# Forgetting attention with two value products a head, and denominators from probabilities summed on VectorE

## What is computed

```python
def fox_prompt(q, k, v, logf):
    c = jnp.cumsum(logf, axis=1)
    ...
        s = jnp.einsum('bqhd,bkhd->bhqk', qi, k).astype(jnp.float32) * ATTN_SCALE
        s = s + (ci[..., None] - cT[:, :, None, :])
        s = jnp.where((kpos[None, :] <= qpos[:, None])[None, None], s, NEG_INF)
        p = jax.nn.softmax(s, axis=-1)
        return jnp.einsum('bhqk,bkhd->bqhd', p.astype(v.dtype), v)
```

## Time and profile before

| what | value |
|---|---|
| median of 3 runs | 1436.95 us (1433.86 to 1438.11) |
| the profiled execution | 1437.47 us, of it span 1435.5 us |
| mean granted TensorE clock | 0.993 of full |
| PE busy | 1390.7 us, 97% |
| DVE busy | 577.2 us, 40% |
| ACT busy | 480.7 us, 33% |
| POOL busy | 213.2 us, 15% |

### The profile page before, as it was taken

How to read it: one execution, slowest core, us unless ns; L and a number is a source line. 1 busy time by engine, 2 the same in 40 slices (tenths; PEclk the granted TensorE clock), 3 DMA queues, 4 the chain that set the end, 5 groups by cost and what they waited for, 6 DMA issues and landing times.

```text
span 1435.5 us, 22601 instructions
## 1 busy us (share of the span) xinstructions
PE 1390.7 (97%) x9041; PEld 1289.6 (90%) x9041; DVE 577.2 (40%) x1378; ACT 480.7 (33%) x1049; POOL 213.2 (15%) x317
## 2 busy tenths in 40 slices
PE   6999999999999799999999999999999999999997
PEld 5989898778888677889999999999999999999997
DVE  6345634232323433563333333343424252525156
ACT  6356655655554552553212121212121212111103
POOL 3145541634343230000000000000000000000000
PEclk9999999999999899999999999999999999999999
DMA  7621125212030443314211120202020202020003
GB/s 197 116 67 38 32 85 160 68 42 79 31 101 8 153 163 132 109 49 118 59 45 48 41 62 28 74 16 74 16 74 16 74 16 74 17 76 20 22 1 121
DMA packets 110255, 97.64 MB, mean 68 GB/s; under 512 B 15936, under 2 KB 96928, under 8 KB 109640
## 3 DMA queue, kind: packets, MB, share of 16 engines
q1 hardware_dynamic: 110152, 96.20, 22.9%
HBM read 77.07 MB, written 19.21 MB: 67 GB/s over the span
## 4 chain that ended last, share of the span: by engine, by line
PE 90%; DVE 3%; DMA 3%; ACT 2%; issue 2%; POOL 1%; SPq 0%; DVEq 0%; ACTq 0%
PE ps L594 27%; PE ps L595 26%; PE ps L596 26%; PE ps L798 2%; PE ps L728 1%; PE ps L945 1%; DMA cb<-c_scratch 1%; PE ps L766 1%; PE ps L810 1%; PE ps L675 1%; DMA ob<-o_scratch 1%; DVE ps L1629 1%; PE ps L889 1%; ACT sp_x L1263 0%; PE ps L608 0%
## 5 line engine op out<-in xcount | busy, mean ns | idle before, releaser
L1876 DVE TENSOR_TENSOR outs<-outs,ps 128x384 f32<-128x384 f32 (+1 forms) x264 | 134.6, 510 | 107.9 <-PE ps L596 107.6
L1862 DVE TENSOR_TENSOR gu<-ps,sg 128x384 f32<-128x384 f32 (+1 forms) x66 | 34.6, 525 | 237.2 <-PE ps L596 237.2
L2046 POOL TENSOR_TENSOR pl_x<-sp_x,ph_x 128x512 fp32r<-128x512 f32 (+5 forms) x120 | 102.0, 863 | 174.4 <-ACT sp_x L1263 172.7
L1443 ACT ACTIVATE h_hi<-gu 128x384 fp32r<-128x384 f32 (+1 forms) x66 | 32.9, 498 | 221.8 <-DVE gu L1862 221.8
L1262 ACT ACTIVATE ph_x<-ps,negc 128x512 fp32r<-128x512 f32 (+5 forms) x120 | 63.0, 525 | 84.3 <-PE ps L810 84.3
L1437 ACT ACTIVATE sg<-ps 128x384 f32<-128x384 f32 (+1 forms) x66 | 30.5, 465 | 171.7 <-PE ps L596 171.7
L594 PE MATMUL ps<-f_hi,ff0hi 128*128 128x384 f32 (+1 forms) x264 | 85.7, 325 | 0.0
L594 PE MATMUL ps<-f_hi,ff1hi 128*128 128x384 f32 (+1 forms) x264 | 85.6, 324 | 0.0
L594 PE MATMUL ps<-f_hi,ff3hi 128*128 128x384 f32 (+1 forms) x264 | 85.6, 324 | 0.0
L594 PE MATMUL ps<-f_hi,ff2hi 128*128 128x384 f32 (+1 forms) x264 | 85.6, 324 | 0.0
L595 PE MATMUL ps<-f_lo,ff0hi 128*128 128x384 f32 (+1 forms) x264 | 85.2, 323 | 0.0
(11 more groups left out here) (311 smaller groups left out, 3775.1 us busy)
## 6 DMA issues: line engine op xcount, KB each, us to landing
raw<-in_w_gate SPq DMA_DIRECT2D x22, 512.0 KB, 4.9
raw<-in_w_up SPq DMA_DIRECT2D x22, 512.0 KB, 4.8
raw<-in_w_down SPq DMA_DIRECT2D x22, 512.0 KB, 4.2
raw<-in_w_in SPq DMA_DIRECT2D x14, 512.0 KB, 4.1
cb<-c_scratch SPq DMA_DIRECT2D x4, 1312.0 KB, 7.4
xt<-in_x_prompt SPq DMA_DIRECT2D x8, 512.0 KB, 4.3
out<-outb SPq DMA_DIRECT2D x16, 256.0 KB, 3.2
ob<-o_scratch SPq DMA_DIRECT2D x16, 256.0 KB, 3.0
```

The lines of the kernel that those rows point to most:

```text
L1443: act.activation(h_hi[par][:, f, c0:c0 + n], gu[(f + c) % 2][:, 0:n], ACT.Copy).then_inc(S["g_hi"], 1)
L1862: dve.tensor_tensor(gu[(f + c) % 2][:, 0:n], bank(3 + c, n), sg[c][:, 0:n], ALU.mult)\
L1876: add = dve.tensor_tensor(y, y, bank(b, whole * P).rearrange("p (t m) -> p t m", t=whole), ALU.add)
L2046: pool.tensor_tensor(pl_x[at][0:rows, 0:n], sp_x[at][0:rows, 0:n], ph_x[at][0:rows, 0:n].bitcast(F32), ALU.subtract).then_inc(S["x_pl"], 1)
```

## The change

The value tile `vw` now has five slots of 64 columns per block: lo values of head 0, hi of head 0, zeros, hi of head 1, lo of head 1. A head's product is two matmuls: its hi and lo slots side by side with `ph_x`, and its hi slot beside the zeros with `pl_x`. Each half of the output rows then holds a part of the same sum, and the two halves are added after the turn, by a reduction on VectorE in place of L1607 and L1611.

The denominators come another way. VectorE adds the full probabilities of all blocks of a chunk in `sum_x` (`fox_sum`, one instruction a head and unit). At a chunk's end ScalarE rounds the sums (`sum_hi`), VectorE forms their remainder (`sum_lo`), and in step j = 4, 12 or 0, part 3, TensorE multiplies both with a 128x128 tile of ones into banks 4 and 5 (`fox_denominators`, four products a chunk; the item "dn"). VectorE takes the reciprocal of the whole banks (`fox_inverses`, 128 by 512 for a head in chunks 0 and 1), and multiplies banks 6 and 7 by it into `ot_x` (`fox_out`, now on VectorE). GpSimd now waits for `fox_sum` instead of the exponential.

```diff
+        if v >= 1 and v <= NX and j in (0, 4, 12):
+            minima(("x", v, 3), "dn", (v - 1) // NFU, {4: 0, 12: 1, 0: 2}[j])
...
+        elif p[0] == "dn":
+            waits.append(("x_rd", 2 * (3 * p[1] + p[2] + 1)))
...
-        (vw_hi, vw_lo), end = lay(outs_at + 4 * D, ("vw_hi", [P, 11, 3, HD], F32R), ("vw_lo", [P, 11, 3, HD], F32R))
+        (vw,), end = lay(outs_at + 4 * D, ("vw", [P, 11, 5, HD], F32R))
+        vw_hi, vw_lo = vw[:, :, 1:4:2, :], vw[:, :, 0:5:4, :]
...
-                    vh, vl = (x[0:rows, vb, h:h + 2, :].rearrange("p s d -> p (s d)") for x in (vw_hi, vw_lo))
+                    both, one = (vw[0:rows, vb, s:s + 2, :].rearrange("p s d -> p (s d)") for s in (3 * h, 1 + h))
                     xh, xl = (x[2 * (v % 2) + h][0:rows, 0:n] for x in (ph_x, pl_x))
-                    product(ps[:, 6 + h, at:at + n], vh, vl, xh, xl, first, last).then_inc(S["x_pv"], 1)
+                    out = ps[:, 6 + h, at:at + n]
+                    pe.matmul(out, both, xh, start=first, stop=False)
+                    pe.matmul(out, one, xl, start=False, stop=last).then_inc(S["x_pv"], 1)
+
+            def fox_denominators(i, c):
+                n, at = FCH[c][1], fox_chunk(i, c)
+                for name, value in bank_free(("dn", i, c)):
+                    pe.wait_ge(S[name], value)
+                pe.wait_ge(S["x_sl"], at + 1)
+                for h in range(2):
+                    pe.matmul(ps[:, 4 + h, 0:n], ones_x[:], sum_hi[:, h, 0:n], start=True, stop=False)
+                    pe.matmul(ps[:, 4 + h, 0:n], ones_x[:], sum_lo[:, h, 0:n], start=False, stop=True)\
+                      .then_inc(S["x_dn"], 1)
...
-            def fox_out(v):
+            def fox_sums_hi(v):
...
+                act.wait_ge(S["x_sum"], 2 * (v + 1))
+                if at >= 1:
+                    act.wait_ge(S["x_dn"], 2 * at)
+                act.activation(sum_hi[:, :, 0:n], sum_x[:, :, 0:n], ACT.Copy).then_inc(S["x_sh"], 1)
...
-                    dve.tensor_tensor(og_x[0:m, 0:tiles, h * HD:(h + 1) * HD], bank_view(b, m, h * HD, [P, tiles], [1, HD]),
-                                      rx_col[0:m, 0:tiles].unsqueeze(2).to_broadcast([m, tiles, HD]), ALU.mult)\
-                       .then_inc(S["ev_dve"], 1)
+                    dve.tensor_reduce(og_x[0:m, 0:tiles, h * HD:(h + 1) * HD], bank_view(b, m, 0, [P, tiles], [1, HD], [HD, 2]),
+                                      mybir.AxisListType.X, ALU.add).then_inc(S["ev_dve"], 1)
...
+            def fox_sum(v):
...
+                    dve.wait_ge(S["x_e"], 2 * v + h + 1)
+                    if first:
+                        dve.tensor_copy(total, p).then_inc(S["x_sum"], 1)
+                    else:
+                        dve.wait_ge(S["x_sum"], 2 * (v - 1) + h + 1)
+                        dve.tensor_tensor(total, total, p, ALU.add).then_inc(S["x_sum"], 1)
...
+            def fox_inverses(i, c):
+                n, at = FCH[c][1], fox_chunk(i, c)
+                for h in range(2):
+                    dve.wait_ge(S["x_dn"], 2 * at + h + 1)
+                    dve.reciprocal(rd_x[:, h, 0:n], ps[:, 4 + h, 0:n]).then_inc(S["x_rd"], 1)
+
+            def fox_out(v):
...
+                for h in range(2):
+                    dve.wait_ge(S["x_pv"], 2 * v + h + 1)
+                    dve.wait_ge(S["x_rd"], 2 * at + h + 1)
+                    dve.tensor_tensor(ot_x[h][:, 0:n], ps[:, 6 + h, 0:n], rd_x[:, h, 0:n], ALU.mult).then_inc(S["x_ot"], 1)
...
-                    pool.wait_ge(S["x_e"], 2 * v + h + 1)
+                    pool.wait_ge(S["x_sum"], 2 * v + h + 1)
```

More of the change, by code:

```diff
@@ L537, in build @@
             w_s w_add w_e w_pl w_m w_ttr w_tm w_es w_pv w_ot w_den og_w0 og_w1
-            x_s x_e x_pl x_m x_ttr x_tm x_pv x_ot x_den x_og ones
+            x_s x_e x_pl x_m x_ttr x_tm x_pv x_ot x_sum x_sh x_sl x_dn x_rd x_og ones
             o_in0 o_in1 o_in2 o_in3 o_in4 o_in5 o_in6 o_in7 o_in8
@@ L1361, in _ @@
                     fox_exp(v)
-                for part in (1, 2, 3):
+                    if FU[v % NFU][8]:
+                        fox_sums_hi(v)
+                for part in (1, 2, 3, 4):
                     items("x", v, part)
-                if 1 <= v <= NX and FU[(v - 1) % NFU][8]:
-                    fox_out(v - 1)
-                items("x", v, 4)
                 for t in SQ_AT.get(v, ()):
@@ L1795, in _ @@
                         values_lo(-1, 3)
-                    for part in range(5):
-                        items("x", v, part)
+                    items("x", v, 0)
+                    items("x", v, 1)
+                    if v < NX:
+                        fox_sum(v)
+                    items("x", v, 2)
+                    if v < NX and FU[v % NFU][-1]:
+                        fox_sums_lo(v)
+                    items("x", v, 3)
+                    if 1 <= v <= NX and FU[(v - 1) % NFU][-1]:
+                        fox_out(v - 1)
+                    items("x", v, 4)
                 if v == ROOT_AT:
```

67 lines of the change are left out of this document (41 added, 26 removed).

## The result

| what | before | changed kernel |
|---|---|---|
| median of 4 runs, side by side | 1436.83 us (1433.86 to 1438.11) | 1501.05 us (1499.98 to 1502.01) |
| ratio, 95% interval | 1 | 1.0432, 1.0411 to 1.0452 |
| mean granted clock | 0.993 | 0.966 |

The change makes the kernel 64 us slower, and the forecast was 1499. The profiled execution of the changed kernel took 1501.53 us, 1499.7 of it span. The page of the changed kernel, busy times first and then the chain that ended last, answers to the earlier trace rows.

A forecast was written before the change was run, and what follows sets the result against it. TensorE, busy for 97% of the span, was taken to bound the kernel, with VectorE (40%) seeming to have room. 1437.47 - 9.5 (gain) + 57.5 (waiting) + 14 (clock) = 1499.5, said as 1499 us; range 1472 to 1530.

The forecast's parts named there:

- TensorE's gain: Forgetting stage: 120 value products fewer save 20.2 us, products with ones add 9.1, less 1.6 for ScalarE: 9.5 us gained.
- The reciprocal: VectorE's reciprocal of a 512-column bank at a chunk's end: 3.3 us, from a slope of 6.2 ns a column.
- The second rival: Reciprocals of 512 columns cost 4.3 us, 1.0 more x 16, giving 1515 us; chance 0.08.
- The new waiting: TensorE waiting for VectorE at chunk ends in the forgetting stage: 57.5 us more, kept at 46 to 62.
- the reductions and short chunks: Turns waiting for VectorE's late reductions, 0.6 to 2.4 us each, and 5.0 us of waits at the four short chunks.
- The clock: TensorE's granted clock falling to half at each of eight new waits of 4 to 7 us: 14 us, kept 0 to 22.
- The first rival: The clock stays full because the waits are spread, giving 1485 us; chance 0.12.
- Banks 4 and 5: TensorE waits because these banks are held until both reciprocals of a chunk are done, 6.7 us for chunks 0 and 1.
- What is hidden: Work off TensorE's path: 120 sum operations (about 53 us) on VectorE, eight ScalarE roundings, GpSimd's later remainder; no added time.
- The third rival: VectorE sums and GpSimd remainders exclude each other at SBUF, delaying some six steps: 1506 to 1507 us; chance 0.07.
- The fourth rival: Not slower: a 512-column reciprocal streams like a subtraction, 0.69 us, giving 1432 us; decides below about 1 us; chance 0.06.
- The verdict: Whole kernel slower by over 0.3%, chance 0.94.

The follow-up runs named there:

- the unread products: Changed kernel with 12 to 24 products of width 512 that nobody reads put before each of TensorE's eight long waits; 1486.1 us, ratio 1.0323.

## Why the prediction was right, and where it was not

**TensorE's gain** (9.5 net). Right, as far as it was measured: 19.3 to 20.0 for the removed products by the kernel without denominators, and 9.6 net as the remainder of the changed one's ledger, good to 2 or 3 us.

**The reciprocal** (3.3 us). Right: 3.321, and 6.2 ns a column again between 256 and 512. The second rival (4.3) falls. The repeat count that the Trainium skill gives on the page "VectorE: DVE Perf Modes", section "First, the fixed hardware budget", read as eight cycles of 0.96 GHz a column, is an estimate of 8.3 ns, and neither width bears it out.

**The new waiting** (57.5). Too large: 46.7, at the lower end of what I kept. The long waits were where the steps said, each a little shorter: 6.30 for 6.4, 6.56 and 6.58 for 6.6, 5.36, 5.35 and 5.35 for 6.4 and twice 5.6, 6.21 for 6.4, and 3.0 (the rest of L704's 9.3) for 3.7. The eight long waits are 44.7 us together, where I had 47.3. The term that failed are the reductions and short chunks. I had put 0.6, 1.5, 1.5 and 2.4 on turns that wait for a reduction, and 5.0 on the short chunks. The waits for `og_x` are 1.7 once and 1.0 once, beside a few tenths, and the largest wait in a short chunk is 1.82. A reduction is a single operation of 0.68, and it was late only where the next turn came at once.

**The clock** (14). Too small: 27 in the ledger, at least 16 by the unread products. I counted eight falls at half to all of 3.4 us, and took off what passes in the wait. There are ten falls. Little passes in the wait: the clock falls inside it, and is down for some 6 us behind its end (2.95 us lost at 274 to 282). And a fall can last far longer: the one at 312 lasted to 332, ten windows, in the kernel before four. The first rival, no clock loss, falls clearly. The price of a whole fall was right: ten falls lost 33.0 us, 3.3 each for my 3.4. What failed was to count half of it.

**Banks 4 and 5.** The places and lengths of the long waits were right, the cause named for them was half right. Freeing the banks early moves the waits to the next thing that VectorE owes, and the time stays.

**What is hidden.** The additions: nearly right, 4 to 5 us in place of 0, although a sum costs 1.02 us and not 0.65 because GpSimd is in the way. The third rival's mechanism is there; its price of 7 us is not, in this order. GpSimd's remainder "nothing, unless a step is shorter": right as the order stands, but without reserve, since moving the sum back in six steps of a pair cost 11 us. I had also written that the trace of the kernel before could not tell whether VectorE and GpSimd hinder each other. It could: of its eight multiplications of 128x1024 at the start (`xn`, two inputs from SBUF), six took 1.28 us, and the two that began inside a GpSimd subtraction, at 20.59 and 31.88, took 1.86 and 1.88.

**The fourth rival** was priced wrongly. Were reciprocals as cheap as a copy, I gave 1432 and a point of decision near 1 us. At 0.68 us the kernel is not faster but 0.27% slower (0.15 to 0.39): idle time grows by 8.8 and clock loss by 7.9, 16.7 in all, against TensorE's gain. I had 5.6 for the waits, and for the clock nothing. Part of the 7.9 belongs to the execution that was profiled: it is 8.0 us above the profiled one of the kernel before, and the medians are 3.9 apart. There is no such length of the reciprocal in what was run at which the change gains.

**The verdict** was right for the reason given: VectorE had 60% of its time free, but not 6.6 us in one piece. That the total came within 2 us owes 11 us of too much waiting and 13 of too little clock to each other.

None of the complete versions beats the kernel before. The two value products alone are worth 17.7 us, and the products with ones, the further hand-overs at each chunk's end and the clock together took more than that in each form tried.

## What to carry to other kernels

An engine with more than half its time free can still be the bound, if work is given to it in pieces longer than the distance between two things that the busy engine wants of it: look for the longest single operation and what is queued behind it, and not for the buffer that it holds. Price a new wait of TensorE with the half clock behind it, which here added some 60% to the idle time and didn't shrink when the waits went from 5 to 7 us down to 3 or 4. Look at the clock behind a row of very narrow products too. Take a reciprocal after a turn, where it has few columns (both forms that did were 40 us faster than the changed kernel), and count each new hand-over between two engines, since even short ones added up to 17 us here.

## What was not expected of the hardware

- The clock's loss did not follow the length of the waits: 33.2 us where the longest was 4.0, 33.0 where it was 6.6, and 13.9 where the waits for the same operations were 1.3 at most and no other was over 2.1.
- It did not need a wait at all: with 16 products of two columns in a row it fell five times behind them while TensorE was busy throughout, and the loss was 26.9 us with no wait over 2.8.
- The kernel was faster with TensorE doing work that nobody reads than with it idle: 164 products more, 16 us less.
- A reciprocal costs the same from SBUF as from PSUM, 3.321 us for 512 columns in both.
- A product of two columns costs 0.11 us with a new stationary side of 128 columns, no less than one of 128 columns.
- A VectorE addition begun beside a GpSimd subtraction of the same width took 1.45 us, alone 0.69, and a subtraction of 256 columns 1.29 in place of 0.42. It shows as a long duration and not as a wait.
